# Sparse attention: the order of two score pairs and two turns in TensorE's program

## The reference, cut to what matters

```python
def dsa_sparse_attention(q, c_kv, w_uk, w_uv, q_idx, k_idx, w_idx):
    ...
        top_val, top_idx = lax.top_k(isc, top_k)
    ...
        s = jnp.einsum('bqhl,bqkl->bqhk', q_lat, c_sel).astype(jnp.float32) * (HEAD_DIM ** -0.5)
        s = s - slopes[None, None, :, None] * dist[:, :, None, :]
        s = jnp.where(sel_ok[:, :, None, :], s, -jnp.inf)
        p = jax.nn.softmax(s, axis=-1)
        o_lat = jnp.einsum('bqhk,bqkl->bqhl', p.astype(c_sel.dtype), c_sel)
        return jnp.einsum('bqhl,lhd->bqhd', o_lat, w_uv)
```

## Time and profile before

| | |
|---|---|
| median of three runs | 3753.74 us |
| profiled execution, its own time | 3756.04 us |
| its span | 3754.2 us |
| TensorE matmul busy, of the span | 3367.8 us (90%) |
| TensorE weight loads | 2916.2 us (78%) |
| VectorE | 2244.1 us (60%) |
| ScalarE | 1954.4 us (52%) |
| GpSimd | 762.5 us (20%) |
| sparse attention, first score to last feed | about 2709 to 3490 us |

### The profile page before, as it was taken

The page is one execution under the profiler, slowest core; times in us unless marked ns, Lnnn a source line. Parts: engine busy times, 40 slices in busy tenths (PEclk is TensorE's granted clock), DMA queues, the critical chain, the costliest instruction groups (busy, mean ns, idle before and its releaser), DMA issues. The chain is left out here.

```text
span 3754.2 us, 91365 instructions
## 1 busy us (share of the span) xinstructions
PE 3367.8 (90%) x36876; PEld 2916.2 (78%) x36876; DVE 2244.1 (60%) x5755; ACT 1954.4 (52%) x4396; POOL 762.5 (20%) x788
## 2 busy tenths in 40 slices
PE   5899999989888879979788999988799988888899
PEld 5777899978777768867566897977677777777687
DVE  7100101037788873320699998969688888888422
ACT  5122211136677762212586667655488888888311
POOL 3222200002577750002004425416100000000000
PEclk9999999999999999989899999999899999999999
DMA  5333421179223223453413354345712222221432
GB/s 191 112 116 113 137 66 65 47 151 251 69 70 81 62 69 135 143 185 119 101 34 118 119 163 140 127 145 213 193 38 81 81 81 81 81 79 40 148 111 83
DMA packets 351756, 416.99 MB, mean 111 GB/s; under 512 B 18920, under 2 KB 256104, under 8 KB 350440
## 3 DMA queue, kind: packets, MB, share of 16 engines
q1 hardware_dynamic: 286584, 318.55, 29.3%
q10 hardware_dynamic: 64768, 92.81, 6.8%
HBM read 247.21 MB, written 164.10 MB: 110 GB/s over the span
## 5 line engine op out<-in xcount | busy, mean ns | idle before, releaser
L1394 PE MATMUL s_o<-s_v,s_pT 128*64 128x64 f32 x13056 | 450.9, 229 | 0.5 <-issue 0.5
L1394 PEld LDWEIGHTS s_o<-s_v,s_pT 128*64 128x64 f32 x13056 | 417.4, 143 | 36.3 <-issue 14.5
L230 PE MATMUL s_acc<-s_wh,s_hT 128*128 128x256 f32 (+1 forms) x1408 | 428.7, 304 | 7.9 <-ACT s_parts L653 4.0
L232 PE MATMUL s_acc<-s_wh,s_hT 128*128 128x256 f32 (+1 forms) x1408 | 428.0, 304 | 0.0
L231 PE MATMUL s_acc<-s_wl,s_hT 128*128 128x256 f32 (+1 forms) x1408 | 428.0, 304 | 0.0
L1551 ACT ACTIVATE s_probs<-s_probs,s_nmx 128x512 f32<-128x512 f32 (+3 forms) x640 | 417.9, 661 | 11.2 <-DVE s_nmx L1597 11.2
L230 PE MATMUL s_acc<-s_hT,s_wh 128*128 128x512 f32 x880 | 349.4, 397 | 57.0 <-DVE s_wl L329 25.7
L1586 DVE CUSTOM_DVE_ANT_0 s_probs<-s_s,s_scores 128x512 f32<-128x512 f32 (+3 forms) x640 | 374.0, 608 | 25.8 <-PE s_s L1366 8.8
L2344 DVE TENSOR_SCALAR_CACHE_REDUCE s_scratch<-s_scores,s_thr 128x384 uint8<-128x384 f32 (+4 forms) x320 | 365.3, 1209 | 1.1
L232 PE MATMUL s_acc<-s_hT,s_wl 128*128 128x512 f32 x880 | 346.7, 394 | 0.0
L231 PE MATMUL s_acc<-s_hT,s_wh 128*128 128x512 f32 x880 | 346.3, 394 | 0.0
(11 more groups left out here) (277 smaller groups left out, 7383.9 us busy)
## 6 DMA issues: line engine op xcount, KB each, us to landing
fm<-s_parts ACTq DMA_DIRECT2D x120, 512.0 KB, 2.8
s_y<-y SPq DMA_DIRECT2D x32, 640.0 KB, 5.8
y<-s_g SPq DMA_DIRECT2D x18, 1024.0 KB, 5.7
kc<-s_parts SPq DMA_DIRECT2D x32, 512.0 KB, 3.4
s_w<-in_o_fm SPq DMA_DIRECT2D x25, 512.0 KB, 4.5
s_w<-in_o_w_in SPq DMA_DIRECT2D x12, 1024.0 KB, 5.3
s_qh<-fm SPq DMA_DIRECT2D x42, 256.0 KB, 3.3
s_ql<-fm SPq DMA_DIRECT2D x42, 256.0 KB, 3.8
```

Of the source, the lines that this page charges most:

```text
L230: nc.tensor.matmul(out, sh, mh, start=(j == 0), stop=False)
L232: ins = nc.tensor.matmul(out, sl, mh, start=False, stop=(j == n - 1))
L1394: last = nc.tensor.matmul(o_ps[half * HD:(half + 1) * HD, 0:HD], pT[half][:, x0:x0 + HD], v[:, g.u.kbs[g.a + x], vc:vc + HD], start=(g.fir ...
```

## The change

In TensorE's program of the sparse attention the second score pair of a batch and the second turn change places. Each batch was: turn, score, score, turn, feeds. It becomes: turn, score, turn, score, feeds. In the last four batches, which have no scores left, nothing changes. The other engines' programs, the number of buffers and all waits stay as they are.

```diff
                 for k in range(0, LEAD, 2):
                     score(k)
                 for n in range(0, NG, BATCH):
-                    turn(n)
-                    if n + LEAD < NG:
-                        score(n + LEAD)
-                        score(n + LEAD + 2)
-                    turn(n + 2)
+                    for a in range(n, n + BATCH, 2):
+                        turn(a)
+                        if a + LEAD < NG:
+                            score(a + LEAD)
                     if n:
                         for x in range(n - BATCH, n):
                             feed(x)
```

## The result

The changed kernel takes 3820.78 us (median of four runs, 3813.6 to 3829.8) against 3753.89 us. The ratio is 1.0176, with a 95% interval of 1.0150 to 1.0202: slower by 67 us, where 3829 us was predicted with a range of 3780 to 3878. The profiled execution took 3813.6 us (span 3811.8), 57.6 more than that of before; the sparse attention lasts from its first score at 2706.3 to the end of its last feed at 3548.8, 842.5 us against 781.5. So the stage's growth of 61.0 us is the whole of it; the rest of the program gave back some 3 us.

A forecast was written before the change was run, and what follows sets the result against it. No engine is full: TensorE, VectorE and ScalarE hand work to each other and wait in turn. Turn delays of 52 us and clock falls of 21 us gave 3756 + 52 + 21 = 3829 us, range 3780 to 3878.

The forecast's parts named there:

- Point 1: In eight waiting batches per head pair, the second turn waits for VectorE's copy, then score follows: 5.35 us per pair.
- Points 2 and 3: Other twelve batches: copy delays turn, three count, 1.35 us per pair lost; ScalarE's earlier copies give back 0.26 us per pair.
- Point 4: Longer waits in batches 0, 2 and 4 lower TensorE's clock: 8 more falls of 2.6 us, 21 us.
- A: Rival: the delay is hidden because VectorE paces the waiting batches; no change, 3750 to 3767 us; chance 0.09.
- B: Rival: the turn fills the eight waits if its copies precede the late bias; 38 us faster, to 3718; chance 0.05.
- D: Rival: clock also falls at waits of batches 6, 8, 12, 15; 83 us plus 10, up to 3922; chance 0.08.
- Signatures: In the profile: turn waits some 100 us, almost none at second score, VectorE's turn waits grown, stage clock 0.92 to 0.93.

The follow-up runs named there:

- e1: New order only in the eight waiting batches (0, 2, 4, 6, 8, 12, 15, 18) of each pair, against the kernel before: 3815.57 us, ratio 1.0168.
- e6: Changed kernel with VectorE's copy cut to 64 columns: 3783.61 us, against 3743.41 us for the old order with the same cut.
- e9: Changed kernel with VectorE's copy for batches 0, 2, 4, 6, 8 moved before the two late biases: 3777.89 us, ratio 1.0069 to the kernel before.
- e10: Kernel before with new order and VectorE's copy moved before the late biases, both only in batches 0, 2, 4, 6, 8: 3757.35 us, ratio 1.0006.
- e11: Kernel before, old order kept, with VectorE's copy for batches 0, 2, 4, 6, 8 moved before the late biases: 3777.54 us, ratio 1.0065.
- e2: New order only in the twelve quiet batches of each head pair, against the kernel before: 3768.24 us, ratio 1.0044.
- e3: Kernel before, old order, with feeds split in halves, two feeds between the two scores of every batch: 3752.73 us, ratio 0.9997.
- e7: Kernel before with feeds moved ahead of the first score, two in batches 0, 2, 4, 8, one in 6, 12, 15, 18: 3718.36 us, ratio 0.9908.
- e8: Kernel before, old order, with two feeds between the two scores only in batches 0, 2, 4 and 8: 3724.82 us, ratio 0.9927.

## Why the prediction was right

**Point 1, the turn behind the copy in the waiting batches: right, 43 us predicted.** By itself (e1) it measures 35.2 us of rest over the runs, and 41 between the profiled stages (834.3 us, of which 50 go to the clock when its share is summed over stretches of 5 us, against 781.5 and 39). Both causes inside it were tested singly: the copy's length (e6) and its place behind the late bias (e9, e10, e11). The term was somewhat too large. It lets batches 2 and 4 lose 0.90 and 0.93 us, above its own cap of 0.69, since the scores there run at the low clock; with the cap it is 4.90 us per pair, 39 in all.

**Points 2 and 3, the quiet batches: right in total, 11 - 2 = 9 us.** e2 measures 8.7 us of rest over the runs, 11 between the profiled stages. The total bears out that most of these delays are swallowed and that all twelve (43 us) do not count; which three of them pay was not measured.

**Point 4, the clock: right in its sign, over in size.** It put 21 us on eight more falls. The profile shows 15 slow feeds instead of 12 and 9 us more of clock share in the stage. Over the runs the share grew by 17.4 us, with a standard error of 4, and it is an upper bound of the cost; that it comes near 21 is in part luck. The terms that were mis-sized are the count and the length of the falls.

Count first. Of the 22 waits of about 2 us and more, 15 have a granted clock under 0.8 over the 6.6 us behind them before (the slow feeds show only 12), and 19 after: four more, not eight. Then length. In 9 of the 15, and 11 of the 19, the mean over these 6.6 us is about 0.75 where a whole fall gives 0.52 to 0.57, so they last about half as long as the one from which 2.6 us was worked out.

"Every lengthened wait is longer than any that now goes unpunished" was said too surely as well. Three lengthened waits of 2.88 to 2.94 us stay at full clock, that of batch 0 above among them, while in e9 and e10 the clock falls behind stops of 1.3 us and less. The length of the last wait alone does not decide; what does stays open.

The spread of the changed kernel's four runs (16 us) goes with their clock share (157 to 172 us).

**The sum:** 52 us of rest predicted and 51.1 measured, with a standard error of 3, and 21 and 17 of clock. It is closer than its terms, so the match to 1 us is chance; the mechanism is not. **The rivals:** A failed in the waiting batches; B's condition, the copy ahead of the bias, did not hold, and when e10 and e11 made it hold the exchange gained 16 us of rest, though not over the kernel before, since the moved copy costs what the turn saves. D's falls at the waits of batches 6, 8, 12 and 15 did not come in the profile.

**Signatures:** the wait moved from the score to the turn as said (79.3 to 1.5). At the turn it is 118 us by the matmuls' row and 168 by the loads', which grew by 130, for "some 100" of the loads. One was misplaced: VectorE's wait for turns grew only by 11 us; most of its growth (from 5.6 to 68.9 us) is a wait for a score. The clock of the stage is 0.94, not 0.92 to 0.93.

## What to carry to other kernels

Before an operation is moved ahead of another, look at what each of them waits for at that place, and where that releaser stands in its own engine's program: here the turn's buffer was freed by a copy that its engine runs just behind the very event for which the score waited, so the turn could not fill that wait, and when that copy was moved forward it did. A delay on an engine costs only where that engine is the next one waited for; count the places one by one, since here eight of twenty batches paid 35 to 41 us and the other twelve, with delays of much the same size, about 10 together. Splitting a long operation to fill waits may cost more than it gives back: e3 put half a feed into every one of them and stayed at the time of before.

## What the runs showed of the hardware

- A feed behind a score starts its loads 0.37 us after the score's last loads, in most batches of the changed kernel. Most of it is no loss: from the woken turn to the feed it is 1.43 us (2907.67 to 2909.10), and score plus turn took 1.38 in the old order (2968.74 to 2970.12). In e3 the same switch, in the middle of a batch, makes the score's slot 0.35 us longer.
- The number of low-clock stretches is a poor measure. e2 has a fall behind each of its 22 long waits, against 15 of 22 before, and its clock share in the stage is only 3 us larger (42 against 39), since all of them are of the short kind, with a mean of 0.74 over the 6.6 us behind the wait.
- Filling TensorE's waits of over 2 us with feeds raised the stage's mean granted clock from 0.95 to 0.99 in e3, e7 and e8. Breaking them with a turn did not do as much: 0.97 in e9 and 0.96 in e10, with slow feeds behind stops of 1.3 us and less.
